# Two-layer hybrid decoder trunk: all sixteen value tiles of attention computed between the head pairs of the indexer

## The chip, the cores and the metric

The kernel runs on one core of a Trainium2 chip. The metric is the device time of one execution in microseconds (us): the median of three runs before the change is 1143.74 (1143.15 to 1146.42). All matrix products are in fp32, most of them as three products of a high and a low part of each operand.

## The reference, cut to what matters

The trunk has two layers over 1024 tokens of width 1024. The change lies in the first of them, in the part that scores keys, and in the projections beside it:

```python
h = rmsnorm(x, pre_norm[layer])
proj = h @ even_w_in[e]
(aq, ak, av, ag, iq, ik, iw, bq, bk, bv, bg, blr) = jnp.split(proj, even_pts, axis=-1)
# for each block of 128 queries:
il = einsum('bthd,bsd->bths', iq_block, ik) * IDX_DIM ** -0.5      # 8 index heads of 64
score = einsum('bth,bths->bts', iw_block, relu(il))                 # "the indexer"
score = where(causal, score, -inf)
_, idx = top_k(score, 256)                                          # attention reads only these keys
# av (1024 tokens x 512): values of the attention; bv (1024 x 512): values of the gated linear attention (GLA)
```

The GLA takes bq, bk, bv and a decay from blr; both mixers are gated by ag and bg, joined, and go through one output projection. Then comes the second layer (recurrent block), which the change doesn't touch.

## The kernel before, in words

Every engine has its own instruction list, written out by hand, and semaphores order them. The names on which the change and the prediction's steps rest:

- **TensorE (PE).** After the normalised input h is turned and the index queries and keys are projected (to about 90 us), PE runs the indexer. It goes over six blocks of queries, `QBS` = 2 to 7 (blocks 0 and 1 hold fewer than 256 keys and need no choice), and in each over four pairs of heads: 24 pairs. `head_scores` (L1661 to L1663) multiplies one pair, two heads side by side in the two halves of the array, three products each over (block + 1) x 128 keys. A pair waits until ScalarE has emptied the bank of the first head of the pair before (`relu_done`).
- **Value tiles.** `token_tile(name, i, t)` projects 128 tokens (t of 8) onto 256 value columns (half i of 2): eight steps k over the width, each the three matmuls of `three` (L1573 to L1575), 24 matmuls of 256 columns. "av" has 2 x 8 tiles, "bv" has 2 x 8. They alternate between banks 0 and 1, and `bank_free` waits for the tile two before to be copied out. In the list `INDEXED`, one whole tile of av half 0 stands behind every third pair. The eight tiles of av half 1 follow the indexer, then `acc_done` is waited for, then the sixteen tiles of bv.
- **ScalarE (ACT).** `relus` empties a head (L853), `values_out` a tile (L860). `high(c)` (L760) rounds the weights of column group c to their high part; c = 4, 5 belong to av half 0, 6 and 7 to av half 1, 8 and 9 to bv half 0, 10 and 11 to bv half 1. high(6) and high(7) stand inside the indexer's list (index 7 and 11), high(8) and high(9) behind it, then the eight copies of av half 1, then high(10) and high(11), then the copies of bv.
- **GpSimd (POOL).** `low(c)` (L605) subtracts the high part from the raw weights. PE's tile waits on `w_lo`. Between these, POOL masks the diagonal of each block of scores once its eight heads are summed (L626). low(6) and low(7) stand behind the second and the third block. Behind the sixth block come two small casts (L639, L640), then low(8), low(9), low(10), ...
- **SyncE (SP).** `load_raw(c)` brings 512 KB into one of two buffers; it waits for `w_lo` of c - 2.
- **VectorE (DVE).** It sums the weighted heads into `score` (L1205, L1208). When all six diagonals are masked it begins the search for the 256th largest score of every row: 31 rounds, each of six counts (L1219, one per block) and two tiny steps on thresholds (L1226, L1228). Into this search other work is written at fixed places (`beside(n)`): at n = 24 the running sums of the gates (L1236 to L1241), at n = 28 and 32 the decayed queries and keys of the GLA (L1246 to L1251, `keys_decayed`; its second call gives `decs_ready` = 2), and from n = 34 on the eight steps of the GLA's state (`gla_step`, L1259 and L1272). n counts half rounds. After the search it makes the masks of the six blocks (L1322 to L1326), in turn with the first attention blocks.
- **The joint.** POOL clears two GLA buffers (L659, L660) after `decs_ready` = 2. PE, which has gone through bv, the decay gates (L1700), the four column groups of bqk and the first two half groups of the output gates, waits for these at `gla_turn(0)` (L1715), and everything behind it on PE waits too. Then PE runs the rest of the gate columns with the GLA's steps between them.

The fp32 memory of bv lies on that of the index queries, which is why bv may not begin before the last head is summed.

Of the kernel before, what the change touches and what calls it, by code (L numbers as in the profile page):

```python
# [25 lines left out]
NT = T // P  # L26
KD = D // P
HALF = 512
A_HEADS, A_DIM = 8, 64
PAIRS = A_HEADS // 2  # L30
# [51 lines left out]
def build(nc, x, rel_bias, pre_norm, post_norm, even_w_in, even_gate_w2, gate_b2, even_w_out,  # L82
# [226 lines left out]
    INDEXED = []  # L309
    for n in range(len(QBS) * PAIRS):  # L310
        INDEXED.append(("score", QBS[n // PAIRS], n % PAIRS))
        if n % 3 == 2:
            INDEXED.append(("av", 0, n // 3))

    small_in = sem("small_in")
    x_in = [sem(f"x_in{t}") for t in range(NT)]
# [273 lines left out]
    def _(pool):  # L590
# [32 lines left out]
        for n, qb in enumerate(QBS):  # L623
            pool.wait_ge(acc_done, A_HEADS * (n + 1))
            diag = score_of(qb)[:, qb * P:(qb + 1) * P]
            pool.affine_select(out=diag, in_=diag, compare_op=ALU.is_ge, fill=NEG, base=0,  # L626
                               pattern=[[-1, P]], channel_multiplier=1).then_inc(diag_done, 1)
            if n in (1, 2):
                low(C_AV + 1 + n)
            if n == 0:  # L630

                pool.memset(low_mask[:, :], 0.0).then_inc(pool_step, 1)
                pool.wait_ge(pool_step, 2)
                for b in range(2):
                    pool.affine_select(out=mask_of(b), in_=mask_of(b), compare_op=ALU.is_ge, fill=NEG, base=b * P,
                                       pattern=[[-1, (b + 1) * P]], channel_multiplier=1).then_inc(mask_low, 1)
# [98 lines left out]
    def _(act):  # L735
# [120 lines left out]
        def values_out(name, s, t):  # L856
            q = nth_product(name, s, t)
            act.wait_ge(proj_full, q + 1)
            dst = v if name == "av" else bv
            act.activation(dst[:, t, s * NEAR:(s + 1) * NEAR], ps[:, q % 2, 0:NEAR], ACT.Copy).then_inc(proj_copied, 1)  # L860

        act.wait_ge(bias_out, 16)
        for i, (name, a, b) in enumerate(INDEXED):
            if name == "score":
                relus(a, b)
            else:
                values_out(name, a, b)
            if i in (7, 11):
                high(C_AV + 2 + (i == 11))
        for c in (8, 9):  # L870
            high(c)
        for t in range(NT):
            values_out("av", 1, t)
        for c in (10, 11):
            high(c)
        for t in range(NT):
# [685 lines left out]
    def _(pe):  # L1562
# [21 lines left out]
        def bank_free(q):  # L1584

            key = PRODUCTS[q - 2]
            if key[0] in BY_DVE:
                pe.wait_ge(proj_free, low_count(*key))
            else:
                pe.wait_ge(proj_copied, copy_count(*key))  # L1590
# [5 lines left out]
            bank_free(q)  # L1596
            weights_first(q % 2, (wH[:, s], wL[:, s]), hf).then_inc(proj_full, 1)

        def token_tile(name, i, t):

            c = {"av": C_AV, "bv": C_BV}[name] + 2 * i
            slot, q = dst_slot(c), nth_product(name, i, t)
            pe.wait_ge(w_lo, c + 2)
            bank_free(q)
            toks = slice(t * P, (t + 1) * P)
            for k in range(KD):
                last = three(ps[:, q % 2, 0:NEAR], (hH[:, k, toks], hL[:, k, toks]),
                             (wH[:, slot:slot + 2, k, :], wL[:, slot:slot + 2, k, :]), k, KD)
            last.then_inc(proj_full, 1)

        pe.wait_ge(w2_in, 48)
        pe.matmul(ps[0:A_HEADS, 7, 0:3 * P], reltab[:, :], nbt[:, :], start=True, stop=True).then_inc(bias_sum, 1)
# [68 lines left out]
            for ins in both:  # L1681
                ins.then_inc(sc_full, 1)

        for name, a, b in INDEXED:
            if name == "score":
                head_scores(a, b)
            else:
                token_tile(name, a, b)
        for name, i in (("av", 1), ("bv", 0), ("bv", 1)):
            if name == "bv" and i == 0:  # L1690
                pe.wait_ge(acc_done, len(QBS) * A_HEADS)
            for t in range(NT):
                token_tile(name, i, t)
# [314 lines left out]
```

## Time and profile before

| | |
|---|---|
| median of three runs | 1143.74 us |
| the profiled execution itself | 1143.6 us, of which the span of instructions is 1141.8 |
| PE busy | 1025.4 us, 90% of the span |
| DVE busy | 704.1 us, 62% |
| ACT busy | 459.8 us, 40% |
| POOL busy | 271.3 us, 24% |
| share of PE on the chain that ended last | 77% (DVE 12%) |
| mean granted TensorE clock | 0.944 of full |

A stretch is worth reading by itself, since the engine that ends it changes: the indexer runs from 90.65 to 161.4 us, av half 1 to 184.4, bv to 230.5, then the decay gates and the bqk columns to 296, the GLA with the output gates to 434, and the masks to 493. A share of 90% says only that PE is nearly always at work, not that each wait of PE is worth its length at the end.

### The profile page before, as it was taken

The numbers are of one execution on the slowest core, as the hardware profiler recorded it, in microseconds if no ns is written. First come the engines' busy times: TensorE is split into PE (matmuls) and PEld (weight loads), VectorE is DVE, ScalarE is ACT, GpSimd is POOL, SyncE is SP. The second block draws the span as 40 slices with busy tenths as digits, with TensorE's granted clock in tenths as the row PEclk, the third lists the DMA queues.
The fourth block names the chain that finished last, engine by engine and source line by source line (L and its number), as shares of the span: only waits on it lengthen the run. The fifth ranks groups of instructions, "written<-read, shape, count | busy, mean of one in ns | idle before, by whom it ended". The sixth has DMA issues, their size and how long they took to land.

```text
span 1141.8 us, 14608 instructions
## 1 busy us (share of the span) xinstructions
PE 1025.4 (90%) x5642; PEld 830.1 (73%) x5642; DVE 704.1 (62%) x1191; ACT 459.8 (40%) x780; POOL 271.3 (24%) x200
## 2 busy tenths in 40 slices
PE   4998889989999998699999655999999999985997
PEld 3876679968777776577777444888788888864886
DVE  5214679998776797865555453456349393958042
ACT  6323552253422234344545542343337272664021
POOL 2210121111323222213221834121232221224100
PEclk8997999989989999799999777999999999988999
DMA  7251111102122222001102224122211111111151
GB/s 235 62 76 30 38 37 39 38 1 56 47 65 77 81 71 86 20 29 38 48 26 104 84 101 148 59 89 92 74 56 56 56 38 56 37 35 60 54 184 74
DMA packets 71306, 75.81 MB, mean 66 GB/s; under 512 B 5016, under 2 KB 58312, under 8 KB 71240
## 3 DMA queue, kind: packets, MB, share of 16 engines
q1 hardware_dynamic: 69968, 73.30, 20.4%
q10 hardware_dynamic: 1272, 1.62, 1.2%
q8 instruction: 43, 0.70, 0.2%
q14 instruction: 23, 0.19, 0.1%
HBM read 58.13 MB, written 16.25 MB: 65 GB/s over the span
## 4 chain that ended last, share of the span: by engine, by line
PE 77%; DVE 12%; ACT 5%; issue 3%; POOL 2%; DMA 1%; DVEq 0%; SPq 0%; POOLq 0%; ACTq 0%
PE ps L1573 21%; PE ps L1574 20%; PE ps L1575 20%; PE ps L1818 3%; PE ps L1802 2%; PE ps L1661 2%; DVE prob L1361 2%; PE ps L1753 1%; PE ps L1663 1%; PE ps L1662 1%; PE ps L1750 1%; ACT relu L853 1%; DVE ysL L1510 1%; PE ps L1721 1%; DVE y L1502 1%
## 5 line engine op out<-in xcount | busy, mean ns | idle before, releaser
L1219 DVE TENSOR_SCALAR_CACHE_REDUCE junk<-score,cand 128x384 bf16<-128x384 f32 (+2 forms) x192 | 169.7, 943 | 1.3
L1573 PE MATMUL ps<-hH,wH 128*128 128x512 f32 x384 | 159.9, 416 | 7.3 <-ACT kdec L887 4.5
L1574 PE MATMUL ps<-hL,wH 128*128 128x512 f32 x384 | 154.3, 402 | 0.0
L1575 PE MATMUL ps<-hH,wL 128*128 128x512 f32 x384 | 153.6, 400 | 0.0
L605 POOL TENSOR_TENSOR wL<-raw,wH 128x1024 fp32r<-128x1024 f32 x32 | 78.3, 2452 | 149.9 <-ACT wH L760 149.9
L1573 PE MATMUL ps<-h1H,w_slot_H 128*128 128x512 f32 x256 | 100.4, 392 | 2.5 <-DVE h1L L1457 2.5
L1575 PE MATMUL ps<-h1H,w_slot_L 128*128 128x512 f32 x256 | 100.1, 391 | 0.0
L1574 PE MATMUL ps<-h1L,w_slot_H 128*128 128x512 f32 x256 | 100.1, 391 | 0.0
L1573 PEld LDWEIGHTS ps<-hH,wH 128*128 128x128 f32 x384 | 74.8, 195 | 29.4 <-issue 14.5
L1575 PEld LDWEIGHTS ps<-hH,wL 128*128 128x128 f32 x384 | 74.7, 195 | 16.8
L1574 PEld LDWEIGHTS ps<-hL,wH 128*128 128x128 f32 x384 | 74.8, 195 | 14.0
L1361 DVE CUSTOM_DVE_ANT_0 prob<-ps,score 128x384 f32<-128x384 f32 (+5 forms) x48 | 42.7, 890 | 61.1 <-PE ps L1802 31.9
L965 ACT ACTIVATE prob<-prob,small 128x128 f32<-128x128 f32 (+7 forms) x64 | 49.7, 777 | 74.4 <-DVE small L1367 74.3
L1573 PE MATMUL ps<-wH,hH 128*128 128x256 f32 x256 | 74.2, 290 | 0.0
L602 POOL TENSOR_TENSOR w_slot_L<-raw,w_slot_H 128x1024 fp32r<-128x1024 f32 x16 | 41.2, 2577 | 137.0 <-ACT w_slot_H L756 137.0
L1574 PE MATMUL ps<-wL,hH 128*128 128x256 f32 x256 | 73.3, 286 | 0.0
L1575 PE MATMUL ps<-wH,hL 128*128 128x256 f32 x256 | 73.2, 286 | 0.0
L1433 DVE RECIPROCAL small<-small 128x1 f32<-128x1 f32 x16 | 2.6, 163 | 108.2 <-ACT small L773 108.2
L1573 PE MATMUL ps<-w2oH,ysH 128*128 128x512 f32 x128 | 50.8, 397 | 12.1 <-DVE silu_g L1496 11.7
L976 ACT ACTIVATE pT<-ps 128x512 f32<-128x512 f32 (+3 forms) x96 | 41.9, 487 | 45.4 <-PE ps L1802 45.4
L1573 PE MATMUL ps<-woH,msH 128*128 128x512 f32 x128 | 51.2, 400 | 8.3 <-POOL msL L717 8.3
L1573 PEld LDWEIGHTS ps<-h1H,w_slot_H 128*128 128x128 f32 x256 | 48.4, 189 | 12.8 <-issue 2.7
(239 smaller groups left out, 2300.4 us busy)
## 6 DMA issues: line engine op xcount, KB each, us to landing
raw<-in_even_w_in SPq DMA_DIRECT2D x32, 512.0 KB, 4.0
xt<-in_x SPq DMA_DIRECT2D x16, 512.0 KB, 5.7
raw<-in_odd_w_in SPq DMA_DIRECT2D x16, 512.0 KB, 4.0
gate_d<-gst SPq DMA_DIRECT2D x16, 256.0 KB, 2.2
raw_row<-in_even_w_out SPq DMA_DIRECT2D x8, 512.0 KB, 3.2
x_d<-xt SPq DMA_DIRECT2D x8, 512.0 KB, 2.6
raw_row<-in_odd_w_out SPq DMA_DIRECT2D x8, 512.0 KB, 3.2
xt<-x_d SPq DMA_DIRECT2D x8, 512.0 KB, 4.7
```

Source lines behind the costliest of these rows:

```text
L602: pool.tensor_tensor(w_slot_L[s][:, :, :], raw[:, c % 2, :, :], w_slot_H[s][:, :, :].bitcast(F32), ALU.subtract).then_inc(w_lo, 1)
L605: pool.tensor_tensor(wL[:, s, :, :], raw[:, c % 2, :, :], wH[:, s, :, :].bitcast(F32), ALU.subtract).then_inc(w_lo, 1)
L965: act.activation(prob[:, i, 0:w], prob[:, i, 0:w], ACT.Exp, bias=nmx[:, c:c + 1], accum_out=lsum[:, c:c + 1]).then_inc(exp_done[e], 1)
L976: act.activation(pT[:, e, 0:m * P], ps[:, TURN_BANK[e], 0:m * P], ACT.Copy).then_inc(turn_out, 1)
L1219: return steps(dve.tensor_scalar(junk1[:, j % 3, 0:(qb + 1) * P], score_of(qb), threshold, None, op, ALU.add, accum_out=dst[:, j:j + 1]))
L1361: dve.tensor_tensor_reduce(out=prob[:, i, 0:w].rearrange("p (b w) -> p b w", b=banks), in0=ps[:, b:b + banks, 0:wb], in1=mask_of(qb).rearr ...
L1573: pe.matmul(dst, lH, rH, start=k == 0, stop=False)
L1574: pe.matmul(dst, lH, rL, start=False, stop=False)
L1575: return pe.matmul(dst, lL, rH, start=False, stop=k == nk - 1)
L1661: yield pe.matmul(ps[:, b + i, 0:wb], qh, kh[:, cols], start=True, stop=False)
L1802: last = pe.transpose(ps[:, TURN_BANK[e], i * P:(i + 1) * P], prob[:, buffer_of(n, e), (first + i) * P:(first + i + 1) * P], ident[:, :])
L1818: both = [pe.matmul(ps[e * A_DIM:(e + 1) * A_DIM, 7, 0:P], v[:, kb, (2 * p + e) * A_DIM:(2 * p + e + 1) * A_DIM], pT[:, e, i * P:(i + 1) * ...
```

## The change

The sixteen av tiles all move into the indexer. Behind each pair PE now does five or six of the products k: five of a tile behind the first pair of three, its last three and two of the next behind the second, the other six behind the third. So two tiles go with three pairs, and the tiles of half 0 and half 1 follow each other. `INDEXED`, by which ACT goes, gets a tile behind the second and the third pair of three. high(6) and high(7) move to index 4 and 9, low(6) and low(7) to the first and second block. ACT's eight copies behind high(9) go away, so high(10) and high(11) come right behind high(8) and high(9).

```diff
     for n in range(len(QBS) * PAIRS):
         INDEXED.append(("score", QBS[n // PAIRS], n % PAIRS))
-        if n % 3 == 2:
-            INDEXED.append(("av", 0, n // 3))
+        if n % 3:
+            INDEXED.append(("av", (2 * (n // 3) + n % 3 - 1) // NT, (2 * (n // 3) + n % 3 - 1) % NT))
...
-            if n in (1, 2):
-                low(C_AV + 1 + n)
+            if n < 2:
+                low(C_AV + 2 + n)
...
-            if i in (7, 11):
-                high(C_AV + 2 + (i == 11))
+            if i in (4, 9):
+                high(C_AV + 2 + (i == 9))
         for c in (8, 9):
             high(c)
-        for t in range(NT):
-            values_out("av", 1, t)
         for c in (10, 11):
             high(c)
...
-        def token_tile(name, i, t):
+        def token_tile(name, i, t, ks=range(KD)):
 
             c = {"av": C_AV, "bv": C_BV}[name] + 2 * i
             slot, q = dst_slot(c), nth_product(name, i, t)
-            pe.wait_ge(w_lo, c + 2)
-            bank_free(q)
+            if ks[0] == 0:
+                pe.wait_ge(w_lo, c + 2)
+                bank_free(q)
             toks = slice(t * P, (t + 1) * P)
-            for k in range(KD):
+            for k in ks:
...
-            last.then_inc(proj_full, 1)
+            if ks[-1] == KD - 1:
+                last.then_inc(proj_full, 1)
...
-        for name, a, b in INDEXED:
-            if name == "score":
-                head_scores(a, b)
-            else:
-                token_tile(name, a, b)
-        for name, i in (("av", 1), ("bv", 0), ("bv", 1)):
-            if name == "bv" and i == 0:
+        for n in range(len(QBS) * PAIRS):
+            head_scores(QBS[n // PAIRS], n % PAIRS)
+            tile = 2 * (n // 3)
+            for u, ks in (((tile, range(5)),), ((tile, range(5, KD)), (tile + 1, range(2))), ((tile + 1, range(2, KD)),))[n % 3]:
+                token_tile("av", u // NT, u % NT, ks)
+        for name, i in (("bv", 0), ("bv", 1)):
+            if i == 0:
                 pe.wait_ge(acc_done, len(QBS) * A_HEADS)
```

## Rows read from the trace of the kernel before

**Rows 1.** Windows: length, busy us (instructions) of PE, PEld, DVE, ACT, POOL, PEclk, DMA, GB/s
```profile
90.60:100.10 9.50, 8.23 (x38) 6.78 (x39) 3.52 (x6) 2.62 (x6) 0.00 (x0) 0.50 0.01 3
100.10:161.40 61.30, 48.70 (x397) 39.47 (x397) 41.73 (x42) 36.44 (x51) 7.43 (x10) 1.00 0.07 18
161.40:184.40 23.00, 23.00 (x194) 23.00 (x193) 22.07 (x54) 4.97 (x10) 5.63 (x5) 1.00 0.18 47
...
230.50:239.90 9.40, 4.91 (x10) 1.54 (x9) 9.19 (x23) 8.34 (x10) 1.93 (x6) 0.65 0.00 1
239.90:243.70 3.80, 3.80 (x9) 2.99 (x10) 3.70 (x11) 3.74 (x4) 0.00 (x0) 0.52 0.02 4
243.70:296.10 52.40, 52.40 (x233) 43.34 (x232) 45.98 (x85) 20.52 (x25) 12.09 (x7) 1.00 0.12 30
296.10:434.20 138.10, 137.18 (x715) 103.11 (x714) 108.33 (x263) 41.20 (x121) 37.88 (x23) 0.98 0.26 78
```

**Rows 2.** Waits of PE, 90.6 to 161.4 us: us in total, times, longest
```profile
PE ps L1661 <- ACT relu L853: 13.8, 16, 1.1
```

**Rows 3.** Chain of waits in the last pairs of the indexer: start, length, what
```profile
148.25 0.32 PE ps L1573
151.30 0.43 PE ps L1661 x2
...
153.99 0.50 PE ps L1661 x2
...
158.41 0.31 PE ps L1573
```

**Rows 4.** Timeline of POOL: start, length, what, idle before and releaser
```profile
162.34 0.29 POOL L626 TENSOR_SCALAR_AFFINE_SELECT score<-score 128x128 f32<-128x128 f32 x1 [12.93 <-DVE score L1208]
...
163.19 4.79 POOL L605 TENSOR_TENSOR wL<-raw,wH 128x1024 fp32r<-128x1024 f32 x2
...
287.02 2.41 POOL L605 TENSOR_TENSOR wL<-raw,wH 128x1024 fp32r<-128x1024 f32 x1 [8.48 <-ACT wH L760]
292.92 0.96 POOL L659 MEMSET att<- 128x1024 f32 x1 [3.49 <-DVE bqk L1251]
293.81 0.31 POOL L660 MEMSET state<- 128x256 f32 x1
...
448.54 2.96 POOL L605 TENSOR_TENSOR wL<-raw,wH 128x1024 fp32r<-128x1024 f32 x1 [1.33 <-ACT wH L760]
```

**Rows 5.** Timeline of ACT at the end of the indexer
```profile
158.45 2.10 ACT L853 ACTIVATE relu<-ps 128x1024 f32<-128x1024 f32 x2 [0.68 <-PE ps L1663]
161.79 2.00 ACT L760 ACTIVATE wH<-raw 128x1024 fp32r<-128x1024 f32 x2
```

**Rows 6.** Timeline of PE: first matmul of bqk, and the first step of the GLA
```profile
239.86 0.77 PE L1573 MATMUL ps<-hH,wH 128*128 128x512 f32 x1 [4.49 <-ACT kdec L887]
...
296.08 0.38 PE L1715 MATMUL ps<-ident,bqk 128*128 128x128 f32 x2
```

**Rows 7.** Timeline of DVE: last heads, search, decayed keys, GLA, masks
```profile
153.97 8.23 DVE L1208 SCALAR_TENSOR_TENSOR score<-relu,wq,score 128x1024 f32<-128x1024 f32 x6 [2.43 <-ACT relu L853]
...
173.77 0.17 DVE L1226 TENSOR_SCALAR rej<-cnt 128x6 int32<-128x6 f32 x1
...
267.59 0.18 DVE L1246 COPY small<-g_a 128x16 f32<-128x16 f32 x1 [5.18 <-ACT g_a L897]
...
287.92 1.54 DVE L1246 COPY small<-g_a 128x16 f32<-128x16 f32 x1 [0.58 <-ACT g_a L897]
...
291.65 1.21 DVE L1251 TENSOR_TENSOR bqk<-bqk,g_d 128x1024 f32<-128x1024 f32 x1
...
305.67 2.97 DVE L1272 SCALAR_TENSOR_TENSOR state<-state,small,ps 64x128 f32<-64x128 f32 x8 [6.41 <-PE ps L1735]
...
449.36 2.70 DVE L1324 SCALAR_TENSOR_TENSOR rank<-rank,need,eqt 128x512 f32<-128x512 f32 x1
```

**Rows 8.** DMA issues of the page: KB each, median us to landing
```profile
raw<-in_even_w_in SPq DMA_DIRECT2D x32, 512.0 KB, 4.0
```

## The prediction

> **What bounds the kernel now.** I read the windows by stage first, then PE's waits, then the timelines of the four engines where the stages meet. In the indexer PE is not full: 8.23 of 9.5 us up to 100.1 and 48.7 of 61.3 us after it. In the 23 us behind it, where av half 1 stands, PE has no gap, and DVE has 22.07 us of work in the same 23, since the search has begun [rows 1]. PE's gaps in the indexer are one kind: 16 waits for the relu of the pair before, 13.8 us, the longest 1.1 [rows 2]. That is what the change can take. But the indexer also feeds DVE: the last head is summed at 153.97 + 8.23 = 162.2, POOL masks the last diagonal, and only then the search starts [rows 4, 7]. The search is DVE's main work up to 434 us, so a later last head is a later search.
>
> Where do the two lines meet? DVE gives the decayed keys at 291.65 + 1.21 = 292.86. POOL clears two buffers behind them to 293.81 + 0.31 = 294.12, and PE's gla_turn(0) comes by at 296.08 [rows 4, 6, 7]. So PE passes the joint 1.96 us after it opens, without a wait. Behind the joint PE is full, 137.18 of 138.1 us [rows 1], and DVE waits for PE (6.41 us at 305.67) [rows 7]. Whatever PE's passing of the joint moves, the end moves with.
>
> **Part 1, the indexer.** A whole tile between pairs takes 151.30 - 148.25 = 3.05 us [rows 3]; its 24 matmuls alone take 24 x 0.12 = 2.88, from 192 matmuls in 23.0 us [rows 1]. So a switch costs about 0.17. Before, 7 tiles stand ahead of the last pair: 21.35 us. After, 23 fillers do: 16 x 2.88, less the last filler's 18 x 0.12 = 2.16, gives 43.92, and 23 x 0.17 = 3.91, together 47.83. Added: 26.5. The 16 waits go, -13.8: the shortest filler is 1.80 + 0.17, longer than the 1.1 of a wait [rows 2].
>
> The clock gives some back. To 100.1 us it stands at half (0.50) with PE in and out of work. In the stretch from 239.9, where PE works without a gap after a stall, half clock lasts 3.8 us and then it is full [rows 1]. The fillers make PE work on from 90.65 without gaps, so I take full clock from 94.5. Before, 8.23 us of work at half clock lost 4.1; after, 3.9 lose 1.95. So -2.1.
>
> Last pair, and with it the last head: 26.5 - 13.8 - 2.1 = +10.6 us. Bounds: with no switch cost +6.7 (which no row makes likely, the 0.17 being measured at whole tiles); with twice the switch cost +14.5; with the clock rising only at 100.1 again +12.7. I take 8 to 13, nearer the 10.6 that the rows give.
>
> A rule bears on the 0.12. The Trainium skill, "TensorE: Matmul & The Clock Gate", section "Back-to-back issue gap", gives N / 2.4 + 2.5 ns, which is 109 ns for 256 columns. This trace doesn't agree: 192 matmuls in 23.0 us are 120 ns [rows 1]. By the rule the 384 value matmuls would take 41.9 instead of 46.1 us and the last head would move by some 2 us less; the row decides.
>
> Can ACT and DVE follow? At the widest block a pair takes 153.99 - 151.30 = 2.69 less its wait of 1.1, near 1.65, and with 1.97 to 2.33 of filler 3.6 to 4.0 us. ACT needs 2.10 for the two relus and on two pairs of three 0.4 for a tile; DVE needs two sums of 8.23 / 6 = 1.37 [rows 3, 5, 7]. Both are hidden. high(6), high(7), low(6) and low(7) come earlier and are needed at the ninth tile, behind the 13th pair; low(7) behind the 8th pair leaves four pairs, over 12 us, for 2.4 us of work. Nothing.
>
> **Part 2, the weights of bv.** Last head at 162.2 + 10.6 = 172.8. POOL's last diagonal, casts and low(8), low(9) end 5.8 us behind the last head (163.19 + 4.79 = 167.98) [rows 4]. Before, that lay beside the eight tiles of av half 1. That cover is gone: bv begins at 178.7, while PE's last filler ends at 158.41 + 10.6 + 2.33 = 171.3 [rows 3]. PE waits 7.4 us. high(8) and high(9) are 2.0 us of ACT right behind the last tile and are not late [rows 5]. bv began at 184.4 before, so PE is 5.7 us early. It restarts at half clock: after the stall of 4.49 us [rows 6], 9 matmuls took 3.8 us where 9 at full clock take 9 x 52.4 / 233 = 2.0 [rows 1], so 1.8 lost. PE is 3.9 us early.
>
> high(10) now stands ahead of the copies of bv and waits for its load, which SP issues when low(8) is done, 176.2; it lands 4.0 later [rows 8], high(10) ends near 181.3. The load for high(11) starts at 178.6, lands at 182.6, and high(11) ends near 183.7. Behind it is the first bv copy, due at 178.7 + 2.9 + 1.8 = 183.4. PE needs that copy only a tile later. Nothing; if the loads took twice 4.0 us, ACT would be late by 4 and PE by some 1 to 2.
>
> **Part 3, the search beside POOL.** DVE's tiny copy at 287.92 took 1.54 us where the same copy took 0.18 at 267.59; it ended at 289.46, POOL's low at 287.02 ended at 289.43. At 449.36 a DVE sum took 2.70 us to 452.06 while POOL's low ran to 451.50 [rows 4, 7]. So some DVE instructions stand still while POOL subtracts. The 1.54 costs 1.36 now, on the line to the joint; after, POOL comes 3.9 earlier (283.1 to 285.5) and DVE later, so it goes. Others come: low(10) and low(11) move to 181.4 to 186.2, and a step of the search falls at 173.77 + 10.6 = 184.4: held 1.8. The running sums and the low of the bqk columns then meet near 262 us, another 0 to 2. I take 2.5 for all that come, between 0 and 5.
>
> The Trainium skill, "SBUF — State Buffer", section "Who interferes with whom", says that a DVE instruction with two SBUF inputs or in a two-port mode and a GpSimd instruction that reads SBUF exclude each other for the whole instruction. The 0.18 against 1.54 agrees [rows 7]. Were it not so, the sum below would be 2.5 lower.
>
> **Part 4, the joint.** DVE waits for ACT twice on the way, 5.18 and 0.58 us [rows 7]. ACT's exponents come with PE, now earlier, so both waits are swallowed. Decayed keys: 10.6 + 2.5 - 5.18 - 0.58 - 1.36 = +6.0, at 298.8; buffers cleared at 300.1. PE arrives at 296.08 - 3.9 = 292.2 and waits 7.9 us. All of PE's gain ends here. It goes on 300.1 - 296.08 = 4.0 us later than before, and again at half clock: +1.8. Sum +5.8.
>
> **Part 5, behind the joint** the order is as before and both lines start together, so I carry +5.8 to the end: 1143.6 + 5.8 = 1149.4. The median of the runs shown stands 0.1 above the profiled execution: 1149.5.
>
> **Rivals.** (a) The lag is mostly swallowed. Last head +8.5 (fillers switch at half the price), holds 0.5: 8.5 + 0.5 - 9.08 (the 7.12 above and the 1.96) = -0.1 at the joint, +1.8 for the clock: 1145.4. For it: 9 us of slack on DVE's line. Against it: the 0.17 stands in the chain.
> (b) The other side, faster: DVE's line has more slack than I see, and PE's early arrival passes the joint. Then PE's 3.9 stay: 1139.8. It decides from where the buffers are cleared before 292.2, that is a last head and holds of under +5.2 together. Against it: 23 us of tiles go ahead of the last head and the waits return 13.8; only with no switch cost and the clock full from the start (-4.1) does it come near.
> (c) Both prices doubled: clock rises late in the indexer (+12.7) and holds of 5: 12.7 + 5 - 9.08 + 1.8 = +10.4: 1154.
>
> **How the numbers follow.** My forecast 0.54, (a) 0.24, (b) 0.10, (c) 0.12. A difference of 0.3%, 3.4 us, is about what a measurement tells from none. Faster is (b), 0.10; the same is (a), 0.24; slower is the forecast and (c), 0.66. The forecast's own range, holds 1 to 4 and last head 9.5 to 12, is 1147 to 1152.5. Down to (a) and up towards (c) the range is 1143.0 to 1153.5.
>
> **What would show it.** Right: no PE waits for relu in the indexer; last head near 173; PE idle 7 us before bv and 5 to 9 us before L1715, released by DVE or POOL; half clock behind both; DVE's 5.18 wait gone. Wrong: a last head before 169; PE arriving at L1715 after the buffers are cleared; a wait that shrinks behind the joint, as DVE's 6.41 would if it lay on DVE's line.

## The result, and the profile after

The changed kernel takes 1154.52 us (median of 6 runs, 1153.14 to 1158.77), the kernel before 1143.66 in the same comparison (6 runs, 1142.19 to 1146.42). The ratio is 1.0097 [1.0078, 1.0117]: slower by 10.9 us. The forecast was 1149.5 with a range of 1143.0 to 1153.5. The direction was right, the size was not: the loss is nearly twice the forecast's and 1 us beyond the range, where rival (c) stood (1154).

The profiled execution of the changed kernel took 1154.42 us with a span of 1152.6. First its page, the busy time of the engines and the chain that ended last:

```profile
PE 1029.1 (89%) x5642; PEld 832.7 (72%) x5642; DVE 711.9 (62%) x1191; ACT 458.9 (40%) x780; POOL 272.9 (24%) x200
...
PE 67%; DVE 23%; issue 3%; ACT 3%; POOL 3%; DMA 1%; DVEq 0%; SPq 0%; POOLq 0%; ACTq 0%
```

PE has 3.7 us more of busy time, but its share of the chain falls from 77% to 67% and DVE's rises from 12% to 23%: some 130 us more of the chain now lie on DVE (0.23 of 1152.6 less 0.12 of 1141.8). The windows of the changed kernel, columns as in [rows 1]:

```profile
90.60:96.00 5.40, 5.17 (x23) 4.51 (x25) 1.04 (x2) 0.87 (x2) 0.00 (x0) 0.50 0.01 3
96.00:98.00 2.00, 2.00 (x14) 1.56 (x13) 0.52 (x1) 0.88 (x2) 0.00 (x0) 0.67 0.00 0
98.00:100.00 2.00, 2.00 (x18) 1.62 (x17) 0.71 (x2) 0.53 (x2) 0.00 (x0) 1.00 0.00 0
...
173.00:184.00 11.00, 4.96 (x28) 4.99 (x29) 10.35 (x26) 3.32 (x5) 7.89 (x6) 0.69 0.37 97
184.00:188.00 4.00, 4.00 (x35) 4.00 (x35) 3.82 (x7) 0.64 (x2) 2.41 (x1) 1.00 0.62 145
...
248.00:304.00 56.00, 44.98 (x199) 36.93 (x197) 55.24 (x101) 18.25 (x22) 12.37 (x5) 0.92 0.11 28
304.00:312.00 8.00, 7.10 (x20) 5.42 (x21) 5.77 (x15) 1.82 (x3) 5.58 (x5) 0.50 0.41 121
312.00:445.00 133.00, 131.86 (x702) 98.96 (x700) 108.13 (x257) 39.14 (x118) 34.64 (x22) 1.00 0.26 77
```

PE is full in the indexer and reaches full clock at about 97. It is idle in two places: from 173 to 184 (the weights of bv) and ahead of 304 (the joint). Behind the joint, from 304.84 to about 312, it works at half clock. PE's waits, 90 to 520 us, in total, times, longest:

```profile
PE ps L1810 <- DVE mixT L1378: 12.8, 4, 5.5
PE ps L1715 <- issue: 11.9, 1, 11.9
PE ps L1571 <- issue: 7.2, 1, 7.2
PE ps L1571 <- ACT kdec L885: 5.3, 1, 5.3
```

The 13.8 us of waits for relu [rows 2] are gone, and 19.1 us of two new ones stand in their place. The timeline of PE at those two places:

```profile
179.04 0.55 PE L1571 MATMUL ps<-wH,hH 128*128 128x256 f32 x1 [7.16 <-issue]
...
304.84 0.66 PE L1715 MATMUL ps<-ident,bqk 128*128 128x128 f32 x2 [11.86 <-issue]
```

Bv begins 5.4 us earlier than before. PE comes to the joint at 292.98, 3.1 us earlier than before [rows 6], and leaves it 8.76 us later than before. Who holds it is seen on POOL's timeline, which answers to [rows 4]:

```profile
173.45 0.29 POOL L626 TENSOR_SCALAR_AFFINE_SELECT score<-score 128x128 f32<-128x128 f32 x1 [14.67 <-DVE score L1206]
...
181.60 4.87 POOL L605 TENSOR_TENSOR wL<-raw,wH 128x1024 fp32r<-128x1024 f32 x2 [2.66 <-ACT wH L760]
...
262.01 3.42 POOL L605 TENSOR_TENSOR wL<-raw,wH 128x1024 fp32r<-128x1024 f32 x1 [8.46 <-ACT wH L760]
...
283.77 3.68 POOL L605 TENSOR_TENSOR wL<-raw,wH 128x1024 fp32r<-128x1024 f32 x1 [8.48 <-ACT wH L760]
303.54 0.95 POOL L659 MEMSET att<- 128x1024 f32 x1 [16.09 <-DVE bqk L1249]
304.43 0.31 POOL L660 MEMSET state<- 128x256 f32 x1
```

The last diagonal comes at 173.45 (before 162.34), the cleared buffers at 304.74 (before 294.12). And DVE's timeline, which answers to [rows 7]; its lines are two numbers lower than before:

```profile
184.79 1.70 DVE L1224 TENSOR_SCALAR rej<-cnt 128x6 int32<-128x6 f32 x1
...
209.24 0.90 DVE L1224 TENSOR_SCALAR rej<-cnt 128x6 int32<-128x6 f32 x1
...
227.16 0.96 DVE L1224 TENSOR_SCALAR rej<-cnt 128x6 int32<-128x6 f32 x1
...
263.26 3.25 DVE L1239 TENSOR_TENSOR g_d<-g_c 128x1024 f32<-128x1024 f32 x1
...
274.80 0.51 DVE L1224 TENSOR_SCALAR rej<-cnt 128x6 int32<-128x6 f32 x1
...
278.21 0.17 DVE L1244 COPY small<-g_a 128x16 f32<-128x16 f32 x1
278.30 1.22 DVE L1245 SCALAR_TENSOR_TENSOR bqk<-bqk,g_a 128x1024 f32<-128x1024 f32 x1
...
285.29 3.25 DVE L1239 TENSOR_TENSOR g_d<-g_c 128x1024 f32<-128x1024 f32 x1
...
299.91 0.17 DVE L1244 COPY small<-g_a 128x16 f32<-128x16 f32 x1
...
302.26 1.22 DVE L1249 TENSOR_TENSOR bqk<-bqk,g_d 128x1024 f32<-128x1024 f32 x1
```

The two waits for ACT ahead of the small copies (L1246 before, L1244 now) are gone: no row has an idle time. But six instructions are longer than usual. The tiny one takes 0.17 when nothing holds it, and the difference of the running sums (L1239) takes 1.22 where nothing holds it, as e3 shows below. Over these they lost 1.53, 0.73, 0.79, 2.03, 0.34 and 2.03: 7.45 us, where before only 1.89 stood between the last diagonal and the joint (most of it the 1.36 that the prediction names). Below, "holds" means such lost time.

### The profile page after: what moved, and what is told of

It is laid out like the page before. It is cut to its first block, busy times and chain, and to the rows that moved or that the text cites. A ratio compares the mean times of both kernels' runs of the same rounds, so it can differ in the third digit from the quotient of the medians.

```text
span 1152.6 us, 14608 instructions
## 1 busy us (share of the span) xinstructions
PE 1029.1 (89%) x5642; PEld 832.7 (72%) x5642; DVE 711.9 (62%) x1191; ACT 458.9 (40%) x780; POOL 272.9 (24%) x200
## 4 chain that ended last, share of the span: by engine, by line
PE 67%; DVE 23%; issue 3%; ACT 3%; POOL 3%; DMA 1%; DVEq 0%; SPq 0%; POOLq 0%; ACTq 0%
PE ps L1571 18%; PE ps L1573 17%; PE ps L1572 17%; DVE junk L1217 8%; PE ps L1818 3%; PE ps L1802 2%; PE ps L1661 2%; DVE prob L1359 2%; PE ps L1662 1%; PE ps L1753 1%; PE ps L1663 1%; PE ps L1750 1%; PE ps L1721 1%; DVE ysL L1508 1%; POOL score L685 1%
## 5 line engine op out<-in xcount | busy, mean ns | idle before, releaser
L1573 PE MATMUL ps<-hH,wL 128*128 128x512 f32 x384 | 153.6, 400 | 0.0
L1571 PE MATMUL ps<-wH,hH 128*128 128x256 f32 x256 | 76.7, 300 | 7.2 <-issue 7.2
L1571 PE MATMUL ps<-w2oH,ysH 128*128 128x512 f32 x128 | 50.8, 397 | 12.1 <-DVE silu_g L1494 11.7
L1571 PEld LDWEIGHTS ps<-wH,hH 128*128 128x128 f32 x256 | 50.0, 195 | 14.6 <-issue 14.6
```

Source lines behind the costliest of these rows:

```text
L1571: pe.matmul(dst, lH, rH, start=k == 0, stop=False)
L1573: return pe.matmul(dst, lL, rH, start=False, stop=k == nk - 1)
```

## The experiments

Two theories stood at first. **A**: PE's passing of the joint sets the end, and the joint opens when DVE's line brings the decayed keys; it is late by the later last head and the holds. **B**: what costs is the lost cover, the 7 us in which PE has nothing behind the indexer, with its half clock. After the first runs came **C**: DVE's whole line from the last head to the end of the search takes a nearly fixed time, so it does not matter at which of the hand-offs between DVE and PE the waiting is done. The C that e4's expectation names is another theory, which is told there. The table has what the profiled executions show (us): the last diagonal (POOL L626), the end of the decayed keys, PE's first GLA matmul with its wait, the end of the search on DVE, the time between the last diagonal and that end, and then two more distances: from the last diagonal to a mark behind the masks, and from the mark to the end of the span. The mark is one instruction of ACT, a softmax of the attention, in the kernel before and in the changed one:

```profile
638.03 0.72 ACT L965 ACTIVATE prob<-prob,small 128x512 f32<-128x512 f32 x1
```

```profile
648.51 0.72 ACT L963 ACTIVATE prob<-prob,small 128x512 f32<-128x512 f32 x1
```

| kernel | last diagonal | decayed keys | joint (wait) | search end | from the diagonal | to the mark | mark to end | median |
| --- | --- | --- | --- | --- | --- | --- | --- | --- |
| before | 162.3 | 292.9 | 296.1 (0) | 434.0 | 271.7 | 475.7 | 503.7 | 1143.7 |
| after | 173.5 | 303.5 | 304.8 (11.9) | 443.0 | 269.5 | 475.1 | 504.1 | 1154.5 |
| e1 | 170.3 | 290.9 | 292.2 (1.1) | 438.4 | 268.1 | 473.5 | 504.0 | 1154.4 |
| e2 | 172.1 | 300.5 | 301.8 (12.1) | 440.5 | 268.4 | 473.8 | 507.9 | 1151.8 |
| e3 | 171.3 | 299.6 | 301.0 (8.4) | 439.4 | 268.1 | 473.5 | 504.7 | 1150.5 |
| e4 | 153.6 | 285.2 | 286.5 (1.1) | 421.3 | 267.8 | 473.2 | 504.4 | 1132.2 |
| e5 | 170.0 | 290.3 | 291.7 (1.1) | 439.1 | 269.2 | 475.8 | 508.2 | 1155.5 |
| e6 | 170.2 | 278.5 | 281.7 (0) | 439.4 | 269.1 | 475.8 | 508.2 | 1158.0 |
| e7 | 162.1 | 295.5 | 296.9 (13.7) | 435.2 | 273.1 | 478.5 | 504.4 | 1147.1 |
| e8 | 162.3 | 293.4 | 296.6 (0) | 444.5 | 282.2 | 489.2 | 508.5 | 1159.6 |
| e9 | 172.0 | 290.8 | 292.2 (1.1) | 432.0 | 259.9 | 466.7 | 508.3 | 1148.6 |
| e10 | 172.8 | 281.8 | 285.0 (0) | 437.7 | 264.9 | 471.2 | 504.2 | 1150.0 |
| e11 | 172.0 | 303.6 | 304.9 (13.7) | 437.1 | 265.1 | 476.9 | 508.3 | 1153.8 |
| e12 | 153.6 | 285.2 | 286.5 (1.1) | 414.8 | 261.2 | 473.1 | 504.5 | 1132.4 |
| e13 | 151.1 | 280.7 | 283.9 (0) | 413.7 | 262.6 | 475.1 | 508.3 | 1132.6 |
| e14 | 171.3 | 297.7 | 299.1 (6.7) | 436.5 | 265.2 | 472.9 | 508.5 | 1153.2 |
| e15 | 154.3 | 286.1 | 287.5 (1.1) | 415.8 | 261.5 | 473.4 | 508.1 | 1130.5 |

The start of the indexer varies from 88.7 to 90.9 between these executions, so 2 us in an absolute time mean little; the distances are free of that. They were timed in four groups, each beside the kernel before: e1 to e4 (before: 1144.0), e5 to e8 (1143.26), e9 to e11 and e13 (1144.14), and e12, e14 and e15 (1142.68). The ratios are to these.

The last distance has two values whatever the edit: 503.7 to 504.7 in eight of the executions, 507.9 to 508.5 in nine. Most of the 4 us arises in the first 100 us behind the mark, where PE does the same 399 matmuls in 70.14 us instead of 65.33 at a lower granted clock; that the clock is all of it isn't shown (e11: 67.73 us, clock 0.76, stretch 98.7). Windows from the mark to a later instruction of ACT (L1011), in the changed kernel, then in e14:

```profile
648.51:743.66 95.15, 65.33 (x399) 52.52 (x400) 37.90 (x87) 35.92 (x64) 39.35 (x27) 0.78 0.28 97
```

```profile
644.21:743.39 99.18, 70.14 (x399) 55.88 (x398) 37.27 (x87) 36.12 (x64) 39.04 (x27) 0.71 0.28 93
```

The profiled executions of e11 and e15, which have the long value, stand 5 and 7 us above their kernels' medians, so it isn't a property of the edit in these. Medians of four runs can differ by some us for this alone, and where such a difference counts below, the distance to the mark is the sharper measure.

### e1: the DVE work beside the search four half rounds earlier

```diff
-            if n == 24:
+            if n == 20:
...
-            if n == 28:
+            if n == 24:
...
-            if n == 32:
+            if n == 28:
```

> The changed kernel, with the running sums and the decayed keys of the GLA put four half rounds earlier into the search (n = 20, 24, 28 instead of 24, 28, 32). Nothing is added or taken away. Theory A (the loss is DVE's late arrival at the joint, L1715): two rounds of 5.7 us leave DVE's line ahead of the joint, the decayed keys come near 292 instead of 303.5, PE no longer waits there (11.9 us now) and keeps full clock behind; the end comes at 1140 to 1143, 11 to 14 us below the changed kernel's 1154.5 and at or below the kernel before. Theory B (the loss is PE's 7.2 us in front of bv and the half clock behind it): PE's work up to the joint is as in the changed kernel, so the time stays at 1153 to 1155.

Measured: 1154.38 us (1149.68 to 1157.30), ratio 1.0097 [1.008, 1.0113], the same as the whole change. (Its profiled execution, 1149.68, is the fastest of the four; its last diagonal came 3.1 us earlier than in the changed kernel's.) The wait at the joint did go, from 11.9 to 1.1. PE's waits in e1, 90 to 520 us:

```profile
PE ps L1721 <- DVE att L1257: 7.2, 1, 7.2
...
PE ps L1715 <- issue: 1.1, 1, 1.1
```

PE now waits 7.2 us at the next hand-off, for DVE's copy of the first att block (n = 34), and the search ends 268.1 us behind the diagonal, where it is 269.5 in the changed kernel. To the mark it is 473.5 instead of 475.1: of 10.8 us less waiting at the joint, 1.5 reach that far. So the wait at the joint by itself is not what sets the end. A's number (1140 to 1143) failed; B's (1153 to 1155) came out, though not for B's reason, as e2 and e7 show.

### e2: the weights of bv inside the indexer

```diff
+            if n in (3, 4):
+                low(C_BV + n - 3)
...
+            if i in (24, 29):
+                high(8 + (i == 29))
```

Their later calls, behind the sixth block, are taken away.

> The changed kernel, with high(8), high(9), low(8), low(9) made inside the indexer (index 24 and 29 of ACT's list, behind the fourth and fifth block on POOL). Theory A: PE's 7.2 us in front of bv shrink to about 2 (the last head stays near 173.3), PE comes some 6 to 8 us earlier to the joint and only waits longer there; the end moves by at most 2 us: 1152 to 1155. Theory B: the 5 to 7 us come back: 1146 to 1149.

Measured: 1151.76 (1149.09 to 1155.57), 1.0057 [1.0036, 1.0078]. PE's gap before bv shrank from 7.2 to 1.5, and its wait at the joint came to 12.1. So 5.7 us given back to PE bring at most 2.8 at the end, and to the mark 1.3; one hold less on DVE is in that too. B, which wanted 1146 to 1149, falls by its size; the number stands just below A's 1152 to 1155.

### e3: the sums off POOL's subtractions

```diff
-            if n == 24:
+            if n == 23:
                 dve.wait_ge(gla_const, 1)
                 gates_summed(0)
             if n == 28:
                 keys_decayed(0)
+            if n == 30:
                 gates_summed(1)
```

> The changed kernel, with the running sums of the gates moved by some half rounds (n = 23 for the first, n = 30 for the second), so that they don't fall on POOL's subtractions at 262 and 284 us; the number of counts ahead of the decayed keys stays. Theory A with the holds as a part of it: L1239 takes 1.22 again instead of 3.25, twice, so the joint and the end come 3 to 4.5 us earlier: 1150 to 1151.5. If DVE isn't really held by POOL, or the joint isn't what counts, L1239 stays long or the time stays at 1154.

Measured: 1150.54 (1149.55 to 1151.72), 1.0053 [1.0036, 1.007]. Both differences of sums are back to 1.22, but the first step of the second sum now meets POOL. DVE's timeline in e3:

```profile
283.94 2.86 DVE L1234 SCALAR_TENSOR_TENSOR kdec<-kdec,g_b 128x1024 f32<-128x1024 f32 x1
286.84 2.29 DVE L1235 TENSOR_TENSOR_SCAN g_c<-reset,kdec 128x1024 f32<-128x1024 bf16 x1
289.16 1.22 DVE L1239 TENSOR_TENSOR g_d<-g_c 128x1024 f32<-128x1024 f32 x1
```

Holds ahead of the joint were 5.85 instead of 7.45, and the joint's wait 8.4 instead of 11.9. A's number (1150 to 1151.5) came out: 4 us of 10.9 came back by moving two calls. But the traces give the holds less of it. At the mark e3 is 3.7 us ahead of the changed kernel, and 2.2 of these it already had at the last diagonal; 1.5 are left for 1.6 us of holds.

### e4: half 0 alone, spread behind the pairs

The other part of the change alone: half 0 in pieces of three, three and two products behind the pairs, half 1 left behind the indexer.

```diff
-        for name, a, b in INDEXED:
...
+        for n in range(len(QBS) * PAIRS):
+            head_scores(QBS[n // PAIRS], n % PAIRS)
+            token_tile("av", 0, n // 3, (range(3), range(3, 6), range(6, KD))[n % 3])
```

> The kernel before, with only the eight av tiles of half 0 in the indexer as before, but spread: three, three and two products k behind the pairs of three. Av half 1 stays behind the indexer and covers the weights of bv. Theory A: the 13.8 us of waits for relu mostly go (a filler of 3 products is 1.08 + 0.17 us against waits up to 1.1), no tile is added ahead of the last head, so the last head comes 8 to 11 us earlier, and PE and DVE both gain it: 1132 to 1137. Theory C (the indexer is at heart bound by DVE and ACT, and filling PE's waits gives nothing): 1141 to 1144.

Measured: 1132.21 (1131.57 to 1132.95), 0.9892 [0.9876, 0.9909], faster than both kernels by 11.8 and 22 us. PE's waits in e4:

```profile
PE ps L1663 <- ACT relu L853: 1.8, 3, 0.9
...
PE ps L1715 <- issue: 1.1, 1, 1.1
```

Eight tiles in pieces fill 12.0 of the 13.8 us. The 16 more switches at 0.17 cost 2.7, so the last diagonal should be 9.3 earlier; it is 8.8 (153.57). The end is 11.8 earlier. So a last head that is *earlier* pays one for one and a little more. A's number (1132 to 1137) came out; that filling PE's waits gives nothing is refuted. What the change moved beyond this, half 1, puts 19.9 us ahead of the last head (173.45 less 153.57) and finds no wait left to fill.

### e5 and e6: all hand-offs early, without and with e2's weights

```diff
-                if n == 34 + 3 * t:     # gla_step
+                if n == 30 + 3 * t:     # e5, with e1's 20, 24, 28
+                if n == 26 + 3 * t:     # e6, with e2's weights and 16, 20, 24
```

> The changed kernel with everything that DVE hands to PE in the GLA put four half rounds earlier into the search: sums and decayed keys at n = 20, 24, 28 (as in e1), and the eight steps of the state from n = 30 instead of 34. In e1 PE passed L1715 after 1.1 us but then stood 7.2 us at L1721 for the first of these steps. Theory A, widened (what counts is the lateness of DVE's whole list, at each hand-off, not the one joint): both waits are gone, PE keeps its 3 to 4 us of earliness, 1139 to 1145. Theory B (the gap in front of bv): 1153 to 1155.

> The changed kernel with the weights of bv made inside the indexer (as in e2) and the hand-offs eight half rounds earlier: n = 16, 20, 24 and from 26. Theory A: now that DVE's lateness doesn't count, the 5 to 7 us in front of bv do: 1134 to 1139. If the gap in front of bv was never worth anything, the time equals e5's.

Measured: e5 1155.49 (1153.58 to 1157.21), 1.011 [1.0091, 1.013]; e6 1158.03 (1155.12 to 1160.12), 1.0137 [1.0112, 1.0163]. No early hand-off helped, and both expectations (1139 to 1145, 1134 to 1139) failed. PE's waits in e5, then in e6:

```profile
PE ps L1661 <- DVE qkL L1347: 9.4, 1, 9.4
```

```profile
PE ps L1663 <- DVE qkL L1349: 22.8, 1, 22.8
```

The att waits are gone and the waiting stands at the end of the search, where PE needs what DVE makes next (qkL). In e6 PE is 23 us early there. In both the search ends 269 us behind the diagonal. This is what made theory C.

### e7: twelve tiles in the indexer, four as cover

```diff
+            token_tile("av", n // 2 // NT, n // 2 % NT, (range(4), range(4, KD))[n % 2])
...
+            for t in range(4 if name == "av" else 0, NT):
```

> The kernel before with twelve av tiles in the indexer, four products k behind each pair, and the last four tiles of half 1 behind it as cover for the weights of bv (they take 11.5 us, 5.8 are needed). Theory A: e4's eight tiles already use up the relu waits, so each further tile puts the last head 3.05 us later: some +11 against e4. PE has no gap in front of bv but waits at L1715 some 6 to 9 us: 1140 to 1145, 8 to 13 above e4. Theory B (the gap in front of bv makes the loss): without the gap the time is e4's, 1131 to 1134.

Measured: 1147.05 (1146.81 to 1147.31), 1.0037 [1.0023, 1.0051]. The four tiles left behind cover the weights of bv: no gap stands there. Still it is 14.8 slower than e4, and PE waits at the joint:

```profile
PE ps L1715 <- issue: 13.7, 1, 13.7
```

With e4 and the change this makes a row of doses: 8, 12 and 16 tiles between the pairs, diagonals at 153.6, 162.1 and 173.5, times 1132.2, 1147.1 and 1154.5. Over both steps the mark moves by 21.7 us for 19.9 of the diagonal, but not step by step: 13.8 for the first 8.6, 7.9 for the next 11.3. So the last head is most of the loss and not all of it. B is refuted here: with no gap at all two thirds of the loss against e4 is there (14.8 of 22.3). The 3.8 us over the kernel before (1143.26 beside it), whose last head stands at the same place, go with holds of 8.7 instead of 1.9 and with the stall at the joint; they were not taken apart further. Both theories' numbers for e7 were too low.

### e8: the kernel before with e5's early hand-offs

```diff
-            if n == 24:
+            if n == 20:
...
-                if n == 34 + 3 * t:
+                if n == 30 + 3 * t:
```

> Control: the kernel before with the hand-offs of e5 (20, 24, 28 and from 30) and nothing else. Theory A: PE already passes the joint without a wait, so 1142 to 1145.5, the kernel before within noise. If moving the hand-offs gives a gain of its own, e5 and e6 have to be read against that.

The other two calls move from 28 and 32 to 24 and 28.

Measured: 1159.58 (1155.54 to 1161.81), 1.0136 [1.0113, 1.0158]. Not expected: in the kernel before, PE has no time to spare at the joint, so DVE asks too early and stands 12.4 us for ACT's exponents; its line grows from 271.7 to 282.2, and PE later waits for the search to end:

```profile
PE ps L1661 <- DVE qkL L1349: 11.4, 1, 11.4
```

The early places cost by themselves when DVE comes to them before PE's results are there. That is why e5 and e6 may not be read as pure removals of a wait.

### e9, e10, e11: the GLA step in two places

`gla_step` first copies att, for which PE waits, then waits itself for PE's states (the 6.41 of [rows 7]). Here the two parts stand two half rounds apart, in e5 (e9), in e6 (e10) and in the changed kernel (e11). E11's form is shown; e9 has 30 and 32, e10 has 26 and 28:

```diff
                 if n == 34 + 3 * t:
-                    gla_step(t)
+                    gla_att(t)
+                if n == 36 + 3 * t:
+                    gla_state(t)
```

> e5 (the changed kernel, hand-offs four half rounds earlier) with each step of the GLA's state split in DVE's list: the copy of the attention block where it was, the four state updates (L1270) two half rounds later, so that DVE counts while PE makes what the updates need. Theory C (since e1, e5 and e8): from the last head to the end of the search DVE's list takes 268 to 272 us in the kernel before, the changed kernel, e4, e5 and e6, of which 20 to 33 are DVE standing still for PE inside the GLA's steps; the end of the search follows the last head one for one, and PE's wait only changes its place. With the standing mostly gone (23 us in e5, under 8 here) the search ends near 425, PE's 9.4 us in front of L1661 go, and the changed kernel's order no longer costs: 1140 to 1146. Theory A alone (the hand-offs): nothing changes against e5, 1154 to 1157.

> e6 (the changed kernel, bv weights inside the indexer, hand-offs eight half rounds earlier) with the same split. Theory C: PE's 22.8 us in front of L1661 shrink by the standing that goes (some 18 us, to 3 to 8), and PE's gain from the filled indexer shows: 1134 to 1141. If DVE's list isn't what ends it: 1156 to 1160 as e6.

> The changed kernel with the split alone, hand-offs where the change left them. PE still waits its 11 to 12 us at L1715 and is full behind it up to the end of the GLA near 444, so by theory C the earlier end of the search (near 425) brings nothing: 1150 to 1155. It tells that both have to go, the wait at the joint and the standing behind it.

Measured: e9 1148.59 (1145.63 to 1150.86), 1.0022 [0.9999, 1.0044]; e10 1150.0 (1148.28 to 1155.26), 1.0049 [1.0029, 1.0069]; e11 1153.82 (1152.52 to 1160.24), 1.0073 [1.0045, 1.0102]. E9 is 6.9 below e5, e10 8.0 below e6: DVE's line is shorter by 9.3 and 4.2, since DVE stands less for PE (12.5 instead of 23.3 us in e9). To the mark e9 takes 9.1 less than e5, the shortest of all kernels. E11 is the other half of this: its search ends 5.9 earlier than the changed kernel's, but its wait at the joint stays (13.7), and it gains nothing, 1153.82 in its expected 1150 to 1155, with 476.9 us to the mark. So either alone is worth nothing here (475.8 us to the mark in e5 and 476.9 in e11, against 475.1), and both together are worth something: in e5 the wait at the joint is gone, in e11 a part of DVE's standing, in e9 both, and e9 is 5.9 below the change with its last head at nearly the same place. That is also the limit of theory C: the line is of fixed length only while DVE stands still inside the GLA's steps. But none beats the kernel before, and the expected numbers of e9 (1140 to 1146) and e10 (1134 to 1141) failed. In e9 the search ended at 432, not 425, and in e10 PE still waits 16.4 us for qkL, where 3 to 8 were expected.

### e12, e13, e15: on from e4

e12 is e4 with the split; e13 and e15 make also the first four and the first two masks right behind the search:

```diff
+        for qb in QBS[:4]:
+            make_mask(qb)
         for f in range(2):
             low_pair_result(0, f)
```

E15 has QBS[:2] here; the same masks are left out of the later loop.

> e4 with the split of the GLA's state steps and nothing else; it separates the two edits of e13. The search ends near 413.7 as in e13, 8 us ahead of PE, and DVE waits for PE there: e4's time, 1131 to 1134. If the split itself costs, it shows here.

> e4 (half 0 spread over the pairs) with the split, and the first four of the six masks made right behind the search, ahead of the first attention results. In e4 the search ends at 421 as PE ends the GLA, and then 60 us are bound by DVE, masks and attention in turn, with PE idle for a quarter. By theory C the search ends some 15 to 18 us earlier with the split, the four masks (17 to 19 us) fit in there, and the stretch of masks shortens by as much: 1114 to 1122. If the search's end doesn't move, the masks only change places: 1130 to 1134.

> e4 with the split and only the first two masks (3.0 and 3.7 us) right behind the search. In e13 the search ended at 413.66, four masks took 16.3 us to 430, and PE, ready near 421, stood 10.2 us at L1661: the gain in the stretch of masks was paid ahead of it. Two masks fit into the 8 us that are free: PE doesn't stand there, the stretch of masks gets 4 to 7 us shorter: 1125 to 1129. If that stretch isn't bound by DVE's sum: 1131 to 1134.

Measured: e12 1132.39 (1131.52 to 1132.97), 0.9908 [0.9891, 0.9925]; e13 1132.57 (1131.88 to 1136.32), 0.9888 [0.986, 0.9916]; e15 1130.47 (1129.67 to 1137.59), 0.9892 [0.9875, 0.9908]. E12 came as expected; the gains that e13 (1114 to 1122) and e15 (1125 to 1129) were to bring are missing. E12's search ends 6.5 earlier than e4's, and nothing of it reaches the end; in e13 the masks take the place. PE's waits, 400 to 520 us, in e4, then in e13:

```profile
PE ps L1810 <- DVE mixT L1380: 12.7, 4, 5.6
```

```profile
PE ps L1669 <- DVE qkL L1353: 10.2, 1, 10.2
PE ps L1816 <- DVE mixT L1384: 5.7, 2, 4.0
```

What the early masks took from the waits for mixT (7.0) they put before the first attention blocks (10.2 instead of 1.5). E4, e12, e13 and e15 can't be told apart: at about 1132 the end of the search no longer sets the end of the kernel.

### e14: both sums free of POOL

It is e3 with the second sum half a round later:

```diff
-            if n == 30:
+            if n == 31:
                 gates_summed(1)
```

> The changed kernel with the first running sum at n = 23 and the second at n = 31, near 287 us, behind POOL's subtraction of 283.8 to 286.2 and ahead of the decayed keys at n = 32. In e3 the second sum, at n = 30, only met POOL with another instruction (L1234 took 2.86 instead of 1.22), so one hold of 2.0 was traded for one of 1.6. Holds as a term of the joint: L1239 and L1234 both take 1.22, from the last head to the decayed keys it is 4 us less than in the changed kernel (130.2), PE waits 8 instead of 11.9 at L1715: 1149 to 1151. If the holds don't count one for one: 1152 to 1155.

Measured: 1153.22 (1151.96 to 1154.54), 1.0089 [1.0072, 1.0106], where less was expected. All steps of both sums were unheld, from the diagonal to the decayed keys it took 126.5 instead of 130.0, and the joint's wait fell to 6.7. So the other branch of the expectation came out, 1152 to 1155, in which the holds don't count one for one. The traces agree with it only in part. At the mark e14 is 4.3 us ahead of the changed kernel, of which it had 2.2 at the last diagonal; 2.1 are left for 3.6 us of holds. The rest of e14's lead is lost behind the mark, in the long value of the last distance (508.5 instead of 504.1), whose windows are shown above the experiments. Whether all four of e14's runs had it isn't known; the medians of e3 and e14, 2.7 apart, don't tell the two kernels apart.

## Why the prediction was wrong

**Part 1 was right.** No wait for relu is left, the clock is full from about 97 (94.5 assumed), the last diagonal is 11.1 later where 10.6 was worked out. The fillers take 1.98 us for 15 matmuls and 2.35 for 18, so a switch costs 0.18 to 0.19 (0.17). The closeness of the sum is in part luck: half clock lasted until about 97.3, so the clock gave back about 1.0 instead of 2.1, and 1 us that nothing in the sum explains went the other way.

**Part 2 was right.** Bv at 179.04 (178.7), PE's wait 7.2 (7.4), full clock again from about 183 on; PE comes to the joint at 292.98 (292.2).

**Part 3 is the step that failed.** "I take 2.5 for all that come, between 0 and 5": it was 7.45, and net of what went 5.6 instead of 1.1. The one that the prediction placed, 1.8 at 184.4, came as 1.53 at 184.79. The meeting of "the running sums and the low of the bqk columns near 262" came too, 2.03. What it left out: the same pair meets a second time 22 us later, because DVE's two sums and PE's column groups (and so POOL's subtractions) are about as far apart (263.26 and 285.29; 262.01 and 283.77), another 2.03; and three tiny steps at 209, 227 and 275 meet POOL, 1.86 together. Each POOL instruction of the stretch should have been laid against DVE's list shifted by 10.6; that was done for two, and even these two cost 3.56, more than the 2.5 set down for all. The Trainium skill, "SBUF — State Buffer", section "Who interferes with whom", has such pairs exclude each other for the whole instruction, in whichever order they come. The trace agrees in both directions: POOL's subtraction at 262.01 began in DVE's scan (to 263.23) and took 3.42 instead of 2.41; DVE's difference at 263.26 then ended 1.08 behind POOL's 265.43.

The sum to the decayed keys: 11.1 + 5.6 - 5.8 (waits for ACT, swallowed as Part 4 said) = 10.9; measured 303.48 - 292.86 = 10.6, predicted 6.0. Two runs test this step. In e14 the holds of the sums are gone and it takes 3.6 us less from the diagonal to the keys, so at the joint their worth is shown. Further on less of it is left: to the mark e3 takes 1.5 us less than the changed kernel (1.6 of holds), e14 2.1 (3.6 of holds). Behind the joint the holds cost nothing that can be seen. DVE loses 5.97 us there instead of 3.50, the most by a second tiny step beside POOL (L1226 at 343.46, 2.27 instead of 0.17), while its standing for PE shrinks from 27.0 to 23.0.

**Part 4** had the mechanism: PE waits, and all its gain ends there. Its wait was 11.9 instead of 7.9, it passed 8.8 later instead of 4.0. The half clock behind it was mis-sized: 1.8 was taken from 3.8 us of half clock; here it lasted some 7 us, and ACT's copies of the output gates, which follow PE, stand 12.1 later than before at 315.72 and 323.88 (before 303.61 and 311.78). So it cost 3.3.

**Part 5**, carried unchanged to the end, was right by a balance of two things it did not have. The kernel before has a stretch of half clock of its own behind the joint that the changed one doesn't repeat. Windows of the kernel before, then of the changed one:

```profile
322.00:329.00 7.00, 7.00 (x24) 5.26 (x21) 4.47 (x13) 1.63 (x9) 0.00 (x0) 0.51 0.08 29
```

```profile
322.00:329.00 7.00, 7.00 (x35) 5.37 (x34) 6.90 (x17) 2.03 (x3) 3.66 (x2) 1.00 0.24 59
```

That gives back 3.1, and the search ends 9.0 later (434.00 and 442.98). Behind it PE's waits for mixT are 1.8 longer (12.8 instead of 11.0), and the difference is 10.8 at the end of the spans (1152.6 - 1141.8): 8.8 + 3.3 - 3.1 + 1.8. That these waits are all of the last 1.8 is read from the sizes and not tested.

**The larger mistake** is one of view. The prediction took PE's passing of the joint as what moves the end, and DVE's wait of 6.41 as proof that DVE has time. E1, e5 and e6 show otherwise: take the wait at the joint away, and it comes up at a later hand-off. (Its own sign, that the 6.41 would shrink if it lay on DVE's line, didn't help: the longest such wait grew to 7.9, while all together fell from 27.0 to 23.0.) From the last diagonal to the end of the search it was 268 to 273 us in all nine kernels up to e7, whether PE waited 0, 1 or 14 us at the joint. DVE stands 20 to 27 us for PE in that time, but the list's order lets neither engine use what the other spares; e9 is the run that shows it, by making both smaller. So the start of the search carries through: the diagonal of the change is 11.1 later, the end 10.9. That the two agree so well is chance, since e7, with the last head where it was before, is 3.8 slower than the kernel before. For rival (a), that the lag is swallowed, it would have needed slack that was no slack. Rival (c) had the right kind, the last head and the holds, and the right time; its terms (12.7 and 5) came as 11.1 and 7.45, so its number owes something to balance too.

Open: why the gains of e12 and of the masks don't show at the end; why the stretch behind the mark has two lengths, and how much of the spread within one kernel (e1: 1149.7 to 1157.3) it makes; and what e7 has beyond its last head.

## What to carry to other kernels

Fill an engine's waits with no more work than the waits hold: 12 of 13.8 us were filled by the eight tiles that were there already, in smaller pieces (1.1% faster), and the tiles beyond them were work put ahead of the next engine's start (with all sixteen, 1.0% slower). Before moving work ahead of a hand-over, ask which list begins at the hand-over and how far it runs in lockstep with the first; a wait on either side in that stretch is not slack until an experiment has shown it. And lay every instruction of the engines that hold each other side by side at the new offset, not only those that met before.

## What of the hardware was not expected

A POOL memset, which reads nothing, also held DVE: the tiny step at 227.16 took 0.96 beside POOL's L646. The changed kernel's POOL timeline:

```profile
227.15 0.95 POOL L646 MEMSET reset<- 128x1024 bf16 x1
```

The granted clock fell to half in the kernel before from 322 to 329 though PE had hardly paused: from 318.3 to 322 it was busy 3.59 of 3.70 us, with the small matmuls of one GLA step. They went on to 323.9, and the rest of the time at half clock were matmuls of 512 columns. The changed kernel kept the full clock over its own steps from 312 to 445 (1.00 in the windows above). The half level behind a stall differs too: it lasted 3.8 us in front of bqk [rows 1] and some 7 us behind the joint, where PE came out of a longer stall (11.9 instead of 4.5 us) and began with 3 us of such small matmuls. The same cost may not be carried from one place to the other.
